# One block from merge to expert queries, two top-16 searches in step, and every fourth value row on TensorE

## The reference

```python
merged = jax.nn.sigmoid(gate_a) * (oa @ w_up_a[l]) + jax.nn.sigmoid(gate_b) * (ob @ w_up_b[l])
y = (merged @ w_o[l]) * gt1[:, None]
x = layer_norm(DN_ALPHA * x + y, ln_g[l, 0], ln_b[l, 0])
hf = x * (1.0 + sc2[:, None]) + sh2[:, None]
y = peer_ffn(hf, w_pq[l], sub_keys[l], peer_u[l], peer_v[l]) * gt2[:, None]
x = layer_norm(DN_ALPHA * x + y, ln_g[l, 1], ln_b[l, 1])
...
q = (h @ w_pq).reshape(B, S, PEER_HEADS, 2, half).astype(jnp.float32)
s1 = jnp.einsum('bshd,hnd->bshn', q[..., 0, :], sub_keys[0].astype(jnp.float32))
s2 = jnp.einsum('bshd,hnd->bshn', q[..., 1, :], sub_keys[1].astype(jnp.float32))
v1, i1 = lax.top_k(s1, PEER_TOPK)
v2, i2 = lax.top_k(s2, PEER_TOPK)
cand = (v1[..., :, None] + v2[..., None, :]).reshape(B, S, PEER_HEADS, PEER_TOPK * PEER_TOPK)
top, pos = lax.top_k(cand, PEER_TOPK)
gates = jax.nn.softmax(top, axis=-1)
...
u = peer_u[ib]
act = jax.nn.gelu(jnp.einsum('btd,bthkd->bthk', hb, u), approximate=False)
return jnp.einsum('bthk,bthkd->btd', gb * act, peer_v[ib])
```

## Time and profile before

| | us |
|---|---|
| median of 3 runs | 4042.52 |
| lowest and highest | 4018.96, 4042.55 |
| the profiled execution's own time | 4049.3 |
| span of the profiled execution | 4047.4 |
| PE busy | 2703.8 (67%) |
| DVE busy | 2649.2 (65%) |
| ACT busy | 995.0 (25%) |
| GpSimd busy | 959.0 (24%) |

### The profile page before, as it was taken

How to read it: one execution, slowest core, us unless ns; L and a number is a source line. 1 busy time by engine, 2 the same in 40 slices (tenths; PEclk the granted TensorE clock), 3 DMA queues, 4 the chain that set the end, 5 groups by cost and what they waited for, 6 DMA issues and landing times. The chain is left out here.

```text
span 4047.4 us, 44570 instructions
## 1 busy us (share of the span) xinstructions
PE 2703.8 (67%) x16804; PEld 2346.9 (58%) x16804; DVE 2649.2 (65%) x3875; ACT 995.0 (25%) x1395; POOL 959.0 (24%) x1028
## 2 busy tenths in 40 slices
PE   6867648948389407776749930000399999996899
PEld 5647427847178406565428830000399899994599
DVE  3624586676777795635686679999755655556454
ACT  2233211010110003232210010000254555543354
POOL 0000015455454460000024447666200000000000
PEclk8978769979699758877769965555699999998699
DMA  6543479999899993533579999999555455550153
GB/s 236 190 165 137 174 286 406 412 386 413 313 387 412 377 360 135 188 125 114 234 286 405 412 350 404 380 379 387 197 169 180 156 174 171 173 176 21 52 169 133
DMA packets 229391, 1034.48 MB, mean 256 GB/s; under 512 B 29672, under 2 KB 32632, under 8 KB 180088
## 3 DMA queue, kind: packets, MB, share of 16 engines
q0 software_dynamic: 147456, 536.94, 34.0%
q1 hardware_dynamic: 81784, 495.51, 33.6%
HBM read 1031.30 MB, written 1.05 MB: 255 GB/s over the span
## 5 line engine op out<-in xcount | busy, mean ns | idle before, releaser
L272 DVE TENSOR_TENSOR w_lo<-raw,w_hi 128x1024 fp32r<-128x1024 f32 (+1 forms) x492 | 557.7, 1138 | 602.1 <-ACT w_hi L259 602.0
L1768 POOL DMA_INDIRECT arena_layer<-in_peer_u,arena_layer x512 | 479.6, 937 | 1576.2 <-SPq L861 1167.1
L1820 DVE CUSTOM_DVE_ANT_0 arena_layer<-arena_layer,ps 128x1024 f32<-128x1024 f32 x512 | 612.7, 1220 | 183.3 <-DMA arena_layer<-in_peer_u,arena_layer 171.5
L1816 DVE SCALAR_TENSOR_TENSOR ps<-arena_layer,ps 128x1024 f32<-128x1024 f32 x512 | 660.3, 1290 | 79.5 <-DMA arena_layer<-in_peer_v,arena_layer 54.2
L650 PE MATMUL ps<-hT_hi,w_hi 128*128 128x256 f32 x2240 | 642.8, 287 | 45.2 <-PEq L791 25.1
L259 ACT ACTIVATE w_hi<-raw 128x1024 fp32r<-128x1024 f32 (+1 forms) x492 | 485.0, 989 | 705.1 <-PE ps L650 703.7
L650 PE MATMUL ps<-hT_lo,w_hi 128*128 128x256 f32 x2240 | 641.1, 286 | 0.0
L650 PE MATMUL ps<-hT_hi,w_lo 128*128 128x256 f32 x2240 | 640.9, 286 | 0.0
L650 PE MATMUL ps<-parts_context,raw 128*128 128x256 f32 x2496 | 549.8, 384 | 58.6 <-PEq L861 58.6
L1768 POOL DMA_INDIRECT arena_layer<-in_peer_v,arena_layer x512 | 479.1, 936 | 331.2 <-DVE ps L1816 313.1
L650 PEld LDWEIGHTS ps<-parts_context,raw 128*128 128x128 f32 x2496 | 482.3, 193 | 125.8 <-issue 59.8
(11 more groups left out here) (339 smaller groups left out, 2959.3 us busy)
## 6 DMA issues: line engine op xcount, KB each, us to landing
raw<-in_ffn_w_gu SPq DMA_DIRECT2D x154, 1024.0 KB
raw<-in_w_mod SPq DMA_DIRECT2D x72, 1024.0 KB
raw<-in_w_ada SPq DMA_DIRECT2D x48, 1024.0 KB
raw<-in_w_in SPq DMA_DIRECT2D x44, 1024.0 KB
raw<-in_ffn_w_down SPq DMA_DIRECT2D x56, 768.0 KB
raw<-in_ffn_w_down SPq DMA_DIRECT2D x56, 640.0 KB
raw<-in_conv_w_in SPq DMA_DIRECT2D x24, 1024.0 KB
raw<-in_w_o SPq DMA_DIRECT2D x8, 1024.0 KB
```

The costliest lines, as they stand in the source:

```text
L272: dve.tensor_tensor(self.lo[:, k, 0:n], self.raw_part(g, parity, k // 2, g.starts(k), g.starts(k + 1)), self.hi[:, k, 0:n].bitcast(F32), A ...
L1768: gp.indirect_dma_start(self.grow[:, slot % GR, :], None, self.tables[slot // half_way], bass.IndirectOffsetOnAxis(ap=self.index[:, k:k + ...
L1816: dve.scalar_tensor_tensor(out=self.tile, in0=row, scalar=cell, in1=self.tile, op0=ALU.mult, op1=ALU.add) \
L1820: dve.tensor_tensor_reduce(row, row, self.tile, 1.0, 0.0, ALU.mult, ALU.add, cell).then_inc(row_used.sem, 1)
```

## The change

Three edits, made together, in both layers.

One: `merge`, `output_projection` and `peer_queries` are registered in one block, and `modulated_features` is no longer called there. The merged features, and the normalised ones, go to PE in four pairs of feature chunks; PE's first tile of each following product waits pair by pair (`ready`, `arrive`). The layer norm's gain and shift are folded into the modulation's scale and shift (`scol`, `bcol`), so that the transposes read the normalised rows (`normed`, in `y_tok`) and `x_tok` itself is made later. The broadcast of the gate row stands ahead of the up-projections. Setup loads `ln_g` and `ln_b` as columns as well.

Two: `top16_pair` takes two lists through the five steps in turn. An instruction waits for the one before the last instead of for the last.

Three: from head `helped` on (the last 5 of 32 in layer 0, the last 16 in layer 1), value rows 3, 7, 11 and 15 of each head are left to PE: ACT makes a diagonal matrix of the row's 128 cells from `ident`, and PE multiplies it by the row in two 512-column matmuls into a second sum in PSUM. GpSimd waits for `row_summed` before it reuses these buffers. At the end of a token tile DVE copies its own sum out and adds PE's (`keep_sum`).

```diff
+            small(vrows[V_LNG:V_LNG + 32, 1, :], a["ln_g"].rearrange("l k (r p) -> (l k r) p", p=P))
+            small(vrows[V_LNB:V_LNB + 32, 2, :], a["ln_b"].rearrange("l k (r p) -> (l k r) p", p=P))
...
+        @block.tensor
+        def _(pe):
+            broadcast_row(pe, lambda c: adacol[:, l, 16 + c:17 + c], 2).then_inc(gate_row_made.sem, 1)
+            for k, src in enumerate((oaT, obT)):
+                if k:
+                    pe.wait_ge(gate_row_kept.sem, gate_row_kept.at(1))
+                project_features(pe, k, lambda b, k=k: ps[:, 2 * k + b // 4,
+                                                          b % 4 * SEQ:(b % 4 + 1) * SEQ], src)
...
+            for pair in range(KC // 2):
+                at = slice(2 * pair, 2 * pair + 2)
+                act.wait_ge(merged.sem, merged.at(pair + 1))
+                act.activation(hT_hi[:, at, :], own[:, at, :], ACT.Copy) \
+                   .then_inc(merged_rounded.sem, 1)
...
+            def split(pair):
+                at = slice(2 * pair, 2 * pair + 2)
+                dve.wait_ge(merged_rounded.sem, merged_rounded.at(pair + 1))
+                dve.tensor_tensor(hT_lo[:, at, :], own[:, at, :], hT_hi[:, at, :].bitcast(F32),
+                                  ALU.subtract).then_inc(merged_split.sem, 1)
+            split_ahead(dve=dve, tile=(0, 0, 0))
+            product_wait(dve, 0)
...
+            for pair in range(KC // 2):
+                at = slice(2 * pair, 2 * pair + 2)
+                src = ps[:, 2 + pair // 2, pair % 2 * 512:(pair % 2 + 1) * 512]
+                v.link(dve.tensor_tensor(other[:, at, :], other[:, at, :],
+                                         src.rearrange("p (b t) -> p b t", t=SEQ), ALU.mult))
+                dve.tensor_tensor(own[:, at, :], own[:, at, :], other[:, at, :], ALU.add) \
+                   .then_inc(merged.sem, 1)
+                if pair:
+                    split(pair - 1)
+                if pair == 2:
+                    split_ahead(dve=dve, tile=(1, 1, 0), quarters=range(HI_EARLY, QUARTERS))
+            split(KC // 2 - 1)
...
+            for t in range(2):
+                project_tokens(pe, t, tiles_of(t), hT, arrive=None if t else ready)
...
+            pe.wait_ge(x_normed.sem, x_normed.at(1))
+            for c in range(KC):
+                turn(0, c)
+            for pair in range(KC // 2):
+                if pair % 2 == 0:
+                    pe.wait_ge(x_normed.sem, x_normed.at(2 + pair // 2))
+                for c in (2 * pair, 2 * pair + 1):
+                    mm = turn(1, c)
+                mm.then_inc(pair_turned.sem, 1)
...
+            for t in range(TT):
+                act.wait_ge(ln_variance.sem, ln_variance.at(t + 1))
+                act.activation(stat[:, 4 + t:5 + t], stat[:, 2 * t + 1:2 * t + 2], ACT.Sqrt,
+                               bias=ln_eps[:]).then_inc(ln_rooted.sem, 1)
+            split_ahead(act=act, tile=(1, 1, 0), quarters=range(HI_EARLY, QUARTERS))
...
+            def residual(t, k):
+                cols = slice(k * 512, (k + 1) * 512)
+                v.link(dve.tensor_tensor(y_tok[:, t, cols], ps[:, k, t * 512:(t + 1) * 512],
+                                         rows[:, 0, cols], ALU.mult))
+                v.link(dve.scalar_tensor_tensor(out=x_tok[:, t, cols], in0=x_tok[:, t, cols],
+                                                scalar=DN_ALPHA, in1=y_tok[:, t, cols],
+                                                op0=ALU.mult, op1=ALU.add))
+                at = 16 + 12 * t + 6 * k
+                v.tick(dve.bn_stats(stat[:, at:at + 6], x_tok[:, t, cols]))
+            split_ahead(dve=dve, tile=(0, 0, 0))
...
+            product_wait(dve, 0)
+            for t in range(TT):
+                residual(t, 0)
+            split_ahead(dve=dve, tile=(1, 1, 0), quarters=range(LO_EARLY))
+            product_wait(dve, 1)
+            for t in range(TT):
+                residual(t, 1)
+                v.wait()
+                dve.bn_aggr(stat[:, 2 * t:2 * t + 2], stat[:, 16 + 12 * t:28 + 12 * t]) \
+                   .then_inc(ln_variance.sem, 1)
+            for t in range(TT):
+                dve.wait_ge(ln_rooted.sem, ln_rooted.at(t + 1))
+                v.link(dve.reciprocal(stat[:, 8 + t:9 + t], stat[:, 4 + t:5 + t]))
+                for part in range(1 + t):
+                    n = D // (1 + t)
+                    cols = slice(part * n, (part + 1) * n)
+                    dve.tensor_scalar(normed[:, t, cols], x_tok[:, t, cols],
+                                      stat[:, 2 * t:2 * t + 1], stat[:, 8 + t:9 + t],
+                                      ALU.subtract, ALU.mult).then_inc(x_normed.sem, 1)
+            for pair in range(KC // 2):
+                dve.wait_ge(pair_modulated.sem, pair_modulated.at(pair + 1))
+                at = slice(2 * pair, 2 * pair + 2)
+                v.link(dve.tensor_copy(hT_hi[:, at, :], full[:, at, :]))
+                dve.tensor_tensor(hT_lo[:, at, :], full[:, at, :], hT_hi[:, at, :].bitcast(F32),
+                                  ALU.subtract).then_inc(pair_split.sem, 1)
+            split_ahead(dve=dve, tile=(1, 1, 0), quarters=range(LO_EARLY, QUARTERS))
+            dve.wait_ge(loaded.sem, loaded.at(32))
+            dve.wait_ge(x_normed.sem, x_normed.at(3))
+            for t in range(TT):
+                v.link(dve.tensor_tensor(x_tok[:, t, :], normed[:, t, :], rows[:, 1, :], ALU.mult))
+                dve.tensor_tensor(x_tok[:, t, :], x_tok[:, t, :], rows[:, 2, :], ALU.add) \
+                   .then_inc(x_renewed.sem, 1)
...
-        def top16(dve, v, values, idx, scores):
-            v.link(dve.max(values[:, 0:8], scores))
-            v.link(dve.max_index(idx[:, 0:8], values[:, 0:8], scores))
-            v.link(dve.match_replace(scores, values[:, 0:8], scores, -3.0e38))
-            v.link(dve.max(values[:, 8:16], scores))
-            v.tick(dve.max_index(idx[:, 8:16], values[:, 8:16], scores))
+        def top16_pair(dve, v, one, other):
+            def both(step):
+                for each in (one, other):
+                    v.tick(step(*each))
+            def both_after(step):
+                for each in (one, other):
+                    dve.wait_ge(vec_step.sem, v.n - 1)
+                    v.tick(step(*each))
+            both(lambda values, idx, scores: dve.max(values[:, 0:8], scores))
+            both_after(lambda values, idx, scores: dve.max_index(idx[:, 0:8], values[:, 0:8], scores))
+            both_after(lambda values, idx, scores: dve.match_replace(scores, values[:, 0:8], scores,
+                                                                    -3.0e38))
+            both_after(lambda values, idx, scores: dve.max(values[:, 8:16], scores))
+            both_after(lambda values, idx, scores: dve.max_index(idx[:, 8:16], values[:, 8:16],
+                                                                scores))
...
+            self.helped = HEADS // 2 if l else HEADS - 5
...
+        def by_tensor(self, slot):
+            return slot // TOPK >= self.helped and slot % SHARE == SHARE - 1
+        def tensor_before(self, slot):
+            return max(0, slot - self.helped * TOPK) // SHARE
+        def vector_before(self, slot):
+            return slot - self.tensor_before(slot)
...
+                left = slot - GR
+                if left < 0:
+                    gp.wait_ge(row_used.sem, row_used.at(slot + 1))
+                elif self.by_tensor(left):
+                    gp.wait_ge(row_summed.sem, row_summed.at(self.tensor_before(left) + 1))
+                else:
+                    gp.wait_ge(row_used.sem, row_used.at(GR + self.vector_before(left) + 1))
...
+            if q > self.helped:
+                dve.wait_ge(row_summed.sem, row_summed.at(self.tensor_before(q * TOPK)))
+                dve.tensor_copy(self.y[:, t, :], self.tile).then_inc(sum_kept.sem, 1)
+                sum_kept.base += 1
+                dve.wait_ge(sum_kept.sem, sum_kept.at(0))
+                ins = dve.tensor_tensor(self.y[:, t, :], self.y[:, t, :], ps[:, t, :], ALU.add)
+            else:
+                ins = dve.tensor_copy(self.y[:, t, :], self.tile)
+            ins.then_inc(tile_in_psum.sem, 1)
...
+            act.copy(self.cells, self.acts[:, at]).then_inc(cells_kept.sem, 1)
+            act.wait_ge(cells_kept.sem, turn + cells_kept.at(q - self.helped + 1))
+            for r in range(SHARED):
+                k = r * SHARE + SHARE - 1
+                act.activation(self.diagonals[:, r, :], ident[:], ACT.Copy,
+                               scale=self.cells[:, k:k + 1]).then_inc(diagonal_made.sem, 1)
+        def shared_rows(self, pe, q, turn):
+            opens = isinstance(turn, int)
+            t, before = q // PEER_HEADS % TT, self.tensor_before(q * TOPK)
+            for r in range(SHARED):
+                k = r * SHARE + SHARE - 1
+                pe.wait_ge(diagonal_made.sem, turn * SHARED + diagonal_made.at(before + r + 1))
```

(15 more changed lines are left out.)

363 lines of the change are left out of this document (213 added, 150 removed).

## The result

| | before | after |
|---|---|---|
| median of the runs, us | 4042.53 (one run more than in the first table) | 3918.59 |
| the profiled execution's own time, us | 4049.3 | 3917.0 |
| span, us | 4047.4 | 3915.2 |

A forecast was written before the change was run, and what follows sets the result against it. DVE was taken to bound lone value rows and selection, gathers the dot-product rows, serial work the stretches between projections. Savings of 50 + 42 + 5 - 1 = 96 us gave factor 0.976, so 3947 us; range 3912 to 3982.

The forecast's parts named there:

- First gap: PE between last up-product and first output product: 14.9 us shrinks to 3.9, as only one pair is awaited.
- The cost of the gate row's broadcast: Broadcast moved ahead of the up-products: costs 1.95 us a layer there, at full clock.
- The slow start behind the gap: First output products on PE at the 1.2 GHz level: 0.5 us of cost taken a layer.
- Second gap: PE between last output product and first query product: 28.9 us shrinks to 12.5, saving 16.4 a layer.
- 0.11 us for a wait, 0.44 a list: DVE's top-16 search: four neighbour waits a list cost 0.11 us each; 0.44 a list, 96 lists, -42 us.
- Rival (a): Search in step gives nothing, since waits are already free; lists keep 1.71 us, total 3989 us; chance 0.07.
- rival (b): In the search only the loads of match values can't overlap: -11 instead of -42 us, total 3978; chance 0.10.
- I take 1.31 us a row: Value rows with PE's help: 1.31 us a row, 21.0 a head, 0.7 saved, 21 heads, -15 us.
- The ends: End of each layer's value sum: PE's late row and DVE's copy and add cost 5.1 us, twice.
- Rival (c): Value rows: the 8 gather buffers bind, landing 7.9 us, PE's hold 3.9; +52 instead of -5, total 4004; chance 0.08.
- Rival (d): Value rows: PE holds buffers longer, in-order gathers stand behind; with a 6 us hold +140, total 4092; chance 0.03.
- Rival (e): More gained: PE holds the fast clock over the first gap and in value rows; 3928 us or less; chance 0.12.

The follow-up runs named there:

- experiment 4: Changed kernel with merge, output projection, modulation and queries in four blocks as before; ratio 0.9886 to the kernel before on the same chip.
- experiment 1: Changed kernel with each top-16 list searched to its end before the next; ratio 0.9894 to the kernel before on the same chip.
- experiment 2: Changed kernel, lists still in step, but each step waits for the instruction just before it; ratio 0.9887 to the kernel before on the same chip.
- experiment 3: Changed kernel with no value rows on PE, DVE taking all; ratio 0.9737 to the kernel before on the same chip.
- experiment 10: Changed kernel again without value rows on PE, on another chip; ratio 0.9773 to the kernel before on the same chip.
- experiment 5: The changed kernel as it is, on another chip; ratio 0.978 to the kernel before on the same chip.
- experiment 8: Changed kernel with the first output and query products waiting for all four pairs; ratio 0.9802 to the kernel before on the same chip.
- experiment 9: The changed kernel as it is, once more on a third chip; ratio 0.9711 to the kernel before on the same chip.
- experiment 11: Changed kernel with four lists in step and PE taking rows 1, 5, 9, 13 of a head; ratio 0.9743 to the kernel before on the same chip.

## Why the prediction was right

**What bounds the kernel** held in all three places: DVE was the bound of the value rows and of the search, and PE's gaps were serial work of DVE.

**Part one** was forecast at -50 and gave -58 (56 in experiment 4). First gap: 3.9 forecast, 3.53 measured. The cost of the gate row's broadcast, 1.95 us, was mis-sized: from PE's first instruction of the block to the last up-product it takes 24.4 us in layer 0 (337.40 - 335.62 = 1.8 of it before the first product) where it took 24.75 without a broadcast, and 26.0 against 24.75 in layer 1. So it costs -0.3 and 1.3 us, since the up-products behind it are shorter. The windows at their start, before and after in layer 0, show the larger part of that (columns as in the earlier trace rows):

```profile
335.40:338.50 3.10, 3.10 (x17) 3.10 (x16) 0.00 (x0) 0.00 (x0) 0.00 (x0) 0.51 0.95 309
```

```profile
337.40:340.00 2.60, 2.60 (x25) 2.60 (x24) 0.00 (x0) 1.02 (x1) 0.00 (x0) 1.00 0.94 244
```

Before, PE had idled 2.74 us and its up-products ran for 3.1 us at the lower level; now it idles as long, but the broadcast comes first and the up-products have the full clock from their start, some 1.5 us less by estimate (half of 3.1). In layer 1 the slow stretch falls mostly into the broadcast, which takes 3.13 us. The slow start behind the gap was under-sized in one layer: the output product takes 0.6 and 1.5 us longer than before, 0.5 forecast. Second gap: 12.5 forecast, 10.45 and 10.75 measured. Its step "7.1 us from first reciprocal to first product", taken from the second network, was too long for this place: it is 397.67 - 391.81 = 5.86 us here, since the second token tile's normalising lies beside the first tile's transposes. The far bound, 57, was just passed.

**Part two** was forecast at -42 and gave -51.4. The mechanism is shown by experiments 1 and 2. The term mis-sized is "0.11 us for a wait, 0.44 a list". The four gaps with a wait, 0.31 to 0.32 us in the earlier trace rows, became 0.19 to 0.20 and not 0.21, which makes 0.48, and the loads and the last gap, which I had left alone, gave the rest of 0.54: small differences, but 96 times. Rival (a), free waits, and rival (b), loads that don't overlap, both fall by the fence of the search. ACT was not late, but nearly: in layer 0 its last modulation copy starts at 534.20 and the second exponential waits 1.68 us for DVE (18.22 before, 7.7 forecast); in layer 1 it waits 12.2. The search stage shrank by all that the lists gave, so by these rows another 2 us off DVE's half would be lost in layer 0.

**Part three** was forecast at -5 and gave -17.5 in the pair of traces that the forecast was for, the far end of its bounds (-17), and nothing in the two pairs on other chips (experiments 3 and 10). In the first pair the step that failed is "I take 1.31 us a row" with its reason, a ring whose landing and hold meet between 1.23 and 1.475. The hold was right at the lower clock (3.75 us a row, 3.9 forecast), and half of the rows had a shorter one, down to 1.98; a head takes 16 gathers at 410 GB/s. So 21 heads gave 25.4 us (21 x 1.21) instead of 15. The ends cost 25.4 - 17.5 = 7.9 instead of 10 to 12: DVE does wait 3.0 to 3.6 us for PE there, but the first heads of each stretch start on rows that have landed already (17.4 to 17.7 us each).

Rival (c), the ring binding through a landing of 7.9 us, did not come: the gathers of this stretch land in 6.3 us in the changed kernel's trace, and a row takes PE 3.8 at most. Rival (d) is not simply gone. One of its steps, that GpSimd issues in order and one buffer held by PE keeps all later gathers waiting, is what the traces on the other chips show: 32 to 41 us of such waits in layer 1 with every fourth row (experiments 1, 2, 4, 5, 8, 9 and 11), 8.9 in the first trace. It cost the gain of part three there, and not the 140 us that the rival reckoned with. The forecast had no term for it, nor for DVE's long changes of head, and that the first pair shows neither is luck: on one of the other chips the -17.5 would have been about nothing. Rival (e), 3928 or less, is what came, by all three parts giving more and not by the clock that it named.

The last 6 us, in the second network, belong to no part, and no run explains them. The two counts of the gain, 124 and 132, differ because the profiled execution of the kernel before lies 7 us above its median.

## What to carry to other kernels

Where short instructions of one engine follow each other on semaphores, put two independent chains in step before anything else: the wait for the instruction just before cost 0.12 of 0.32 us here, and two chains recover all of it. When an engine is relieved, ask first at what rate the next bound runs, and then which engine will hold the shared buffers and how late it may pass them on: the same edit was worth 17 us in one pair of traces and nothing in two others, where what DVE lost no more was lost waiting for PE. And cut each trace into stages at landmarks before comparing kernels; a stage that no edit touches moved by 22 us here.
